# Cross attention with a feature-major product with V, and a head-major forget gate with a running sum

## What is computed

```python
for l in range(DEPTH_2):                                   # 2 layers
    x = x + 0.5 * swiglu(rmsnorm_2(x, g_ffn1[l]), ...)
    h = rmsnorm_2(x, g_mix[l])
    z = h @ w_mix_in[l]                                    # ... and 8 forget columns zf
    log_f = log_sigmoid(zf + b_f[l])
    y_att = forgetting_attention(q, k, v, log_f)           # c = cumsum(log_f) over the tokens
    x = x + y @ w_mix_out[l]
    x = x + memory_cross_attention(rmsnorm_2(x, g_xattn[l]), rmsnorm_2(mem, g_mem[l]), ...)
    x = x + 0.5 * swiglu(rmsnorm_2(x, g_ffn2[l]), ...)

def memory_cross_attention(h, m, w_q, w_kv, w_o):          # 4 heads of 256, 256 memory rows
    s = einsum('bshd,bmhd->bhsm', q, k) * (XHEAD_DIM ** -0.5)
    p = softmax(s, axis=-1)
    o = einsum('bhsm,bmhd->bshd', p, v).reshape(B, S, D_MODEL)
    return o @ w_o
```

## Time and profile before

| | |
|---|---|
| median of 3 runs | 1566.6 us (1564.68 to 1567.84) |
| profiled execution | 1566.79 us, of which the span from first to last instruction is 1564.5 us |
| mean granted TensorE clock | 0.993 of 2.4 GHz |
| PE busy | 1541.5 us (99% of the span) |
| PEld busy | 1349.5 us (86%) |
| DVE busy | 967.6 us (62%) |
| ACT busy | 756.3 us (48%) |
| POOL busy | 50.2 us (3%) |

### The profile page before, as it was taken

The page is one execution under the profiler, slowest core; times in us unless marked ns, Lnnn a source line. Parts: engine busy times, 40 slices in busy tenths (PEclk is TensorE's granted clock), DMA queues, the critical chain, the costliest instruction groups (busy, mean ns, idle before and its releaser), DMA issues.

```text
span 1564.5 us, 22731 instructions
## 1 busy us (share of the span) xinstructions
PE 1541.5 (99%) x8810; PEld 1349.5 (86%) x8810; DVE 967.6 (62%) x992; ACT 756.3 (48%) x839; POOL 50.2 (3%) x76
## 2 busy tenths in 40 slices
PE   9999999999999999999999999999999999999997
PEld 8888888888888899989888887888899989888886
DVE  4556766657665745765666666666664666476665
ACT  5544544446444534544544445444445444364444
POOL 0210000000000000000100000000000000000000
PEclk9999999999999999999999999999999999999999
DMA  9544455455555454343455554555544354255552
GB/s 364 191 153 176 159 190 193 180 188 194 196 181 196 148 213 162 135 162 135 162 188 188 188 188 171 203 179 198 192 168 182 120 177 174 97 183 193 181 194 108
DMA packets 39640, 279.57 MB, mean 179 GB/s; under 512 B 4368, under 2 KB 4624, under 8 KB 6160
## 3 DMA queue, kind: packets, MB, share of 16 engines
q1 hardware_dynamic: 38848, 275.27, 48.4%
q10 hardware_dynamic: 720, 3.29, 0.6%
HBM read 277.49 MB, written 1.05 MB: 178 GB/s over the span
## 4 chain that ended last, share of the span: by engine, by line
PE 97%; DVE 1%; issue 1%; DMA 0%; ACT 0%; POOL 0%; POOLq 0%; ACTq 0%; DVEq 0%
PE ps L338 95%; PE ps L523 2%; PE ps L553 0%; DMA res<-x_in 0%; DVE res L1436 0%; DVE Pb L1416 0%; PE ps L532 0%; DVE PTb L1413 0%; PE ps L513 0%; ACT Pb L1226 0%; DVE qk_tok L1775 0%; POOL stat L1805 0%; DVE Vx L1383 0%; DVE xmax L1757 0%; PE ps L850 0%
## 5 line engine op out<-in xcount | busy, mean ns | idle before, releaser
L1257 DVE TENSOR_TENSOR w_lo<-raw,w_hi 128x2048 fp32r<-128x2048 f32 x252 | 576.4, 2291 | 321.1 <-ACT w_hi L889 320.7
L338 PE MATMUL ps<-xT,w_hi 128*128 128x512 f32 (+1 forms) x2984 | 727.7, 345 | 0.0
L889 ACT ACTIVATE w_hi<-raw 128x2048 fp32r<-128x2048 f32 (+1 forms) x255 | 484.6, 1900 | 361.3 <-PE ps L338 347.7
L338 PEld LDWEIGHTS ps<-xT,w_hi 128*128 128x128 f32 x2984 | 478.9, 191 | 20.8
L338 PE MATMUL ps<-xT,w_lo 128*128 128x256 f32 x2304 | 478.5, 281 | 0.0
L338 PEld LDWEIGHTS ps<-xT,w_lo 128*128 128x128 f32 x2304 | 409.0, 190 | 53.8
L338 PE MATMUL ps<-w_hi,sT_hi 128*128 128x512 f32 x576 | 185.8, 391 | 0.8 <-DVE Vx L1383 0.8
L338 PE MATMUL ps<-w_hi,xT 128*128 128x512 f32 (+2 forms) x640 | 186.3, 385 | 0.0
L338 PE MATMUL ps<-w_lo,sT_hi 128*128 128x512 f32 x576 | 184.9, 390 | 0.0
L338 PE MATMUL ps<-w_hi,sT_lo 128*128 128x512 f32 x576 | 184.8, 390 | 0.0
L338 PEld LDWEIGHTS ps<-w_hi,xT 128*128 128x128 f32 x640 | 118.1, 193 | 24.3 <-issue 1.3
(11 more groups left out here) (165 smaller groups left out, 848.3 us busy)
## 6 DMA issues: line engine op xcount, KB each, us to landing
raw<-stream_in SPq DMA_DIRECT2D x256, 1024.0 KB, 4.8
kTx<-mem_in ACTq DMA_DIRECT2D x2, 1024.0 KB, 6.5
res<-x_in SPq DMA_DIRECT2D x2, 512.0 KB, 5.8
kTx<-mem_in SPq DMA_DIRECT2D x1, 1024.0 KB, 9.3
cu<-gate_bias_in SPq DMA_DIRECT2D x1, 1024.0 KB, 14.5
qk_tok<-post_gain_in ACTq DMA_DIRECT2D x1, 1024.0 KB, 5.0
out<-Vx SPq DMA_DIRECT2D x2, 512.0 KB, 3.1
cst<-consts_in SPq DMA_DIRECT2D x1, 512.0 KB, 7.7
```

The source lines that it names most:

```text
L338: return nc.tensor.matmul(bank_ap, lh, rh, start=start, stop=stop)
L889: nc.scalar.activation(w_hi[:, slot(c), 0:width], raw[:, slot(c), 0:width], copy).then_inc(unit_hi, 1)
L1257: nc.vector.tensor_tensor(w_lo[:, slot(c), :], raw[:, slot(c), :], w_hi[:, slot(c), :].bitcast(F32), sub).then_inc(unit_lo, 1)
```

## The change

In the cross attention the probabilities are divided by their sums before they are transposed (`x_norm` on DVE: one reciprocal of two columns and two in-place multiplications of 128 x 256 a head), the product with V puts out features by tokens straight into the banks 0 to 3 (`x_values`: V stationary, 256 tokens moving, again 16 float32 products), and `turn(xq_tok)`, `xo0`, `xo1` and the tile `xq_tok` are gone. `turn_round` and `turn_rest` read the banks 0 to 3, and the `tall` units and `onto_res` use the banks 4 to 7. The work of the heads is interleaved on PE and DVE. ACT copies the heads 2 and 3 to `PTb`, DVE the heads 0 and 1.

In the forget gate the weights become the stationary operand: ACT writes the 8 rounded columns of each row block at steps of 64 in `w_hi`, DVE the rest 32 columns behind, and 16 products with 256 tokens moving give heads by tokens in bank 4 (rounded weights in partitions 0 to 7, rests in 32 to 39). The bias becomes a column (`bcol`). The elementwise steps run on 8 partitions x 256 tokens, in `PTb`. The sum over the tokens is a `tensor_tensor_scan` on DVE (`cum`), and the two products with `upto` are gone. `cT` is set to zero once at the start.

The name of the change also speaks of a merged gate/up; `merged` stands in the kernel before already, and the diff does not touch it.

PE:

```diff
@@ -678,6 +691,7 @@
+            pe.wait_ge(set_ready, 3)
             with pe.Fori(0, LAYERS) as l:
@@ -737,16 +751,10 @@
                 pe.wait_ge(unit_lo, upto_unit(L3, m0 + 4))
-                fw = w_hi[:, slot(m0 + 4), 0:F_COLS].rearrange("p (k n) -> p k n", k=KT)
                 for k in range(KT):
-                    for t in range(TOK):
-                        def hi_pass(o=ps[:, 4 + t, 0:2 * HEADS], x_=xT_hi[:, k, t * P:(t + 1) * P]):
-                            return mm(o, x_, fw[:, k, :], k == 0, k == KT - 1)
-                        if k < KT - 1:
-                            hi_pass()
-                        last = mm(ps[:, 4 + t, 0:HEADS], xT_lo[:, k, t * P:(t + 1) * P], fw[:, k, 0:HEADS], False, False)
-                        if k == KT - 1:
-                            last = hi_pass()
+                    fw = w_hi[:, slot(m0 + 4), k * F_STEP:k * F_STEP + P]
+                    mm(ps[:, 4, 0:S], fw, xT_hi[:, k, :], k == 0, False)
+                    last = mm(ps[:, 4, 0:S], fw, xT_lo[:, k, :], False, k == KT - 1)
                 last.then_inc(unit_used, 1)
...
                 flipped(L3, m0 + 7, 0, B)
-                wait_dve("logf")
-                mm(ps[:, 6, 0:S], nlf[:, 0, :], upto, True, False)
-                mm(ps[:, 6, P:S], nlf[:, 1, :], upto[:, 0:P], False, True).then_inc(l_pe.sem, l_pe.one("cT"))
                 flipped(L3, m0 + 8, 1, B)
                 wait_dve("cT")
...
+                def x_turn(h):
+
+                    wait_dve(f"xn{h}")
                     for m in range(2):
                         for t in range(TOK):
                             last = nc.tensor.transpose(ps[:, 4 + h, m * S + t * P:m * S + (t + 1) * P],
                                                        Pb[:, h, t * S + m * P:t * S + (m + 1) * P], ident)
                     last.then_inc(l_pe.sem, l_pe.one(f"PX{h}"))
...
-                                last = mm(ps[:, 2 * half + t, e * XDH:(e + 1) * XDH],
-                                          PTb[:, h, m * S + t * P:m * S + (t + 1) * P],
-                                          Vx[:, m, h * XDH:(h + 1) * XDH], m == 0, m == 1)
-                    last.then_inc(l_pe.sem, l_pe.one(f"OX{half}"))
-
-                def o_wait(k):
-                    if k % 4 == 0:
-                        wait_dve(f"xo{k // 4}")
-                turn(xq_tok, N, wait=o_wait)
+
+                def x_values(h):
+
+                    if h < 2:
+                        wait_dve(f"PX{h}")
+                    else:
+                        wait_act(f"PX{h}")
+                    for d in range(2):
+                        for m in range(2):
+                            last = mm(ps[:, h, d * S:(d + 1) * S], Vx[:, m, h * XDH + d * P:h * XDH + (d + 1) * P],
+                                      PTb[:, h, m * S:(m + 1) * S], m == 0, m == 1)
+                    last.then_inc(turn_T, 1)
+
+                x_scores(0)
+                x_scores(1)
+                x_scores(2)
+                x_turn(0)
+                x_scores(3)
+                x_turn(1)
+                x_values(0)
+                x_turn(2)
+                x_values(1)
+                x_turn(3)
+                x_values(2)
+                x_values(3)
                 tl = turns_before(l, 4)
                 for i in range(4):
-                    tall(L3, m0 + 29 + i, 2 * i, 0, i == 0, i == 3, xT_hi, xT_lo, tiles=tl)
+                    tall(L3, m0 + 29 + i, 2 * i, 4, i == 0, i == 3, xT_hi, xT_lo, tiles=tl)
```

ACT:

```diff
-                wait_pe("cT")
-                did(nc.scalar.activation(cT[:], ps[:, 6, 0:S], copy), "cT_hi")
+                wait_dve("cum")
+                did(nc.scalar.activation(cT[0:HEADS, :], f_cum[0:HEADS], copy), "cT_hi")
...
-                for h in (0, 2):
+                for h in (2, 3):
                     wait_pe(f"PX{h}")
                     did(nc.scalar.activation(PTb[:, h, :], ps[:, 4 + h, :], copy), f"PX{h}")
-                turn_round(turns_before(l, 4), N, None)
+                turn_round(turns_before(l, 4), (0, 1, 2, 3), None)
```

DVE:

```diff
+                did(nc.vector.tensor_tensor_reduce(out=bpick[:], in0=ident[:, 0:HEADS], in1=colsL[:, L_BF:L_BF + HEADS],
+                                                   scale=1.0, scalar=0.0, op0=mul, op1=add, accum_out=bcol[:]), "bcol")
                 unit(5)
...
+                did(nc.vector.tensor_tensor(f_lo[hi], ps[lo, 4, 0:S], inv_row[lo, :], mul), "f_lo")
+                did(nc.vector.tensor_tensor(f_hi[hi], ps[hi, 4, 0:S], inv_row[hi, :], mul), "f_hi")
+                wait_own("f_hi")
+                did(stt(out=f_all[hi], in0=f_hi[hi], scalar=bcol[hi], in1=f_lo[hi], op0=add, op1=add), "f")
                 wait_own("f")
-                did(stt(out=lf[:, 1], in0=lf[:, 0], scalar=-1.0, in1=lf[:, 0], op0=mul, op1=mx), "fabs")
+                did(stt(out=f_abs[hi], in0=f_all[hi], scalar=-1.0, in1=f_all[hi], op0=mul, op1=mx), "fabs")
                 unit(7)
 
                 wait_act("fln")
...
+                did(stt(out=f_neg[hi], in0=f_all[hi], scalar=0.0, in1=f_ln[hi], op0=ALU.min, op1=sub, reverse1=True), "logf")
+                wait_own("logf")
+                did(nc.vector.tensor_tensor_scan(f_cum[hi], ones[hi, 0:1].to_broadcast([HEADS, S]), f_neg[hi], 0.0, mul, add),
+                    "cum")
                 unit(8)
                 unit(9)
                 wait_act("cT_hi")
-                did(nc.vector.tensor_tensor(cT[32:64, :], ps[32:64, 6, 0:S], cT[32:64, :].bitcast(F32), sub), "cT")
+                did(nc.vector.tensor_tensor(cT[lo, :], f_cum[hi], cT[hi, :].bitcast(F32), sub), "cT")
...
+                def x_norm(h):
+
+                    wait_act(f"xexp{h}")
+                    did(nc.vector.reciprocal(rinv[:, h:h + 9:8], soft[:, 1, h:h + 9:8]), f"xr{h}")
+                    wait_own(f"xr{h}")
+                    for t in range(TOK):
+                        pr = Pb[:, h, t * S:(t + 1) * S]
+                        last = nc.vector.tensor_scalar(pr, pr, rinv[:, 8 * t + h:8 * t + h + 1], None, mul)
+                    did(last, f"xn{h}")
...
+                x_shift(0)
+                x_shift(1)
+                x_norm(0)
+                x_shift(2)
+                x_norm(1)
+                x_turned(0)
+                x_shift(3)
+                x_norm(2)
+                x_turned(1)
+                x_norm(3)
+                turn_rest(turns_before(l, 4), (0, 1, 2, 3), None)
                 for i in range(31, 34):
                     unit(i)
-                onto_res(3, (L3, m0 + 32), 0, lambda t: 1.0)
+                onto_res(3, (L3, m0 + 32), 4, lambda t: 1.0)
```

More of the change, by code:

```diff
@@ L44 @@
 F_COLS = KT * 2 * HEADS
+F_STEP, F_LOW = 64, 32
 WARM_X, WARM_FIRST, WARM_NORM = 3, 3, 7
@@ L143, in program @@
         rinv = sb("rinv", [P, 16])
-        lf = sb("lf", [P, 5, TOK, HEADS])
+        bcol = sb("bcol", [P, 1])
+        bpick = sb("bpick", [P, HEADS])
         nlf = sb("nlf", [P, TOK, P])
@@ L164, in program @@
         zbT = zb_tok[:, :, :].rearrange("p t n -> p (t n)").rearrange("p (c n) -> p c n", c=4)
-        xq_tok = qk_tok[:, :, :, :].rearrange("p a t n -> p (a t n)").rearrange("p (t n) -> p t n", t=TOK)
         xqT = qkT[:, :, :, :].rearrange("p a k n -> p (a k) n")
         mem_tok = kTx[:, :, :].rearrange("p k n -> p (k n)").rearrange("p (t n) -> p t n", t=TOK)
+        f_lo, f_hi, f_all, f_abs, f_exp, f_ln, f_neg, f_cum = (
+            PTb[:, i // 2, (i % 2) * S:(i % 2) * S + S] for i in range(8))
         o_tok, ysq = q_tok, k_tok.rearrange("p t n -> p (t n)").rearrange("p (c n) -> p c n", c=4)
@@ L289, in upto_unit, with forget_cols, forget_raw @@
             return r3 * RING + c + 1
+        def forget_cols(w, c):
+            return w[:, slot(c), 0:KT * F_STEP].rearrange("p (k n) -> p k n", k=KT)
+        def forget_raw(c):
+            return raw[:, slot(c), 0:F_COLS].rearrange("p (k n) -> p k n", k=KT)[:, :, 0:HEADS]
         @block.sync
@@ L835, in _, with x_scores @@
                 flipped(L3, m0 + 28, 1, B, half_sem=l_pe.sem)
-                for h in range(XH):
+                def x_scores(h):
                     if h == 0:
@@ L1156, in _ @@
                 unit(3)
-                round_unit(L3, m0 + 4, F_COLS)
+                act.wait_ge(unit_landed[slot(m0 + 4)], landed(L3, m0 + 4))
+                used(L3, m0 + 1)
+                nc.scalar.activation(forget_cols(w_hi, m0 + 4)[:, :, 0:HEADS], forget_raw(m0 + 4), copy).then_inc(unit_hi, 1)
                 unit(5)
@@ L1161, in _ @@
                 wait_dve("fabs")
-                did(nc.scalar.activation(lf[:, 2], lf[:, 1], exp, scale=-1.0), "fexp")
+                did(nc.scalar.activation(f_exp[0:HEADS], f_abs[0:HEADS], exp, scale=-1.0), "fexp")
                 act.wait_ge(l_act.sem, l_act.upto("fexp", l))
-                did(nc.scalar.activation(lf[:, 3], lf[:, 2], ACT.Ln, bias=1.0), "fln")
+                did(nc.scalar.activation(f_ln[0:HEADS], f_exp[0:HEADS], ACT.Ln, bias=1.0), "fln")
```

(35 more changed lines are left out.)

37 lines of the change are left out of this document (7 added, 30 removed), and 3 rows, old and new, of the table L_DVE.

## The result

The changed kernel takes 1550.71 us in the median of 4 runs (1547.77 to 1550.93) against 1566.25 us for the kernel before (4 runs, 1564.68 to 1567.84). The ratio is 0.9895, with a 95% interval of 0.9884 to 0.9907. The forecast was 1551.0 us. The profiled execution is the fastest of the four, 1547.77 us with a span of 1546.0 us, 18.5 us shorter than the span before. The other three take 3 us more; their mean granted clocks, 0.995 to 0.997 against 0.996, do not explain it, and none of them was profiled. Experiment 9 ran the same kernel again and took 1548.65 us in the median.

A forecast was written before the change was run, and what follows sets the result against it. PE was taken to bound the kernel, with 97% of the chain that ended last. The terms 6.3 + 3.3 + 4.9 + 1.3 = 15.8 us, off the profiled 1566.8 us, gave 1551.0 us; range 1547.5 to 1556.5.

The forecast's parts named there:

- Cross attention: Stage from first score to first `tall`: 16.01 us instead of 19.16, 3.15 us less a layer, 6.3 us in all.
- upper bound of 3.4 us a layer: Cross-attention stage: the gain without any wait of PE or cost for changing the kind of product, 3.4 us.
- Forget products: Forget block: 16 products in 1.92 us instead of 32 in 3.59; 1.67 us saved a layer, 3.3 in all.
- The clock: Behind the forget block: the fall to 1.2 GHz goes, saving 1.65 us in layer 0 and 3.25 in layer 1, 4.9.
- The sum over tokens: Forget gate: the two products with `upto` go, 0.65 us a layer, 1.3 in all; the scan is costed at nothing.
- 6.6 was counted: Forget gate: about 6.6 us left for DVE's scan after `logf` before PE would feel it.
- the clock falls all the same: Rival, behind the new forget block: the fall in clock and its 4.9 us stay, 1555.9 us; chance 0.12.
- DVE's chain: Rival, cross attention: transposes wait for DVE's divisions, some 1.5 us a layer stay as new waits, 1554.0 us; chance 0.10.
- its rival: Start of layer 1: pause or clock differs, about 1548.0 us if the clock holds, 1554 to 1557 with second pause; chance 0.08.
- The slower rival: Forget gate: the scan is far slower than elementwise, costing beyond 6.6 us; at 17 us the kernel takes 1571.8; chance 0.02.

The follow-up runs named there:

- experiment 9: The changed kernel itself run once more, with no edit, on the same chip as the version with the load moved: 1548.65 us.
- Experiment 1: The kernel before with only the cross-attention part of the change, forget gate as before: 1559.5 us, ratio 0.9958.
- experiment 3: The kernel before with each of the forget block's 32 products streaming 256 columns instead of 16 or 8: 1560.93 us, ratio 0.9967.
- Experiment 2: The kernel before with only the forget-gate part of the change, cross attention as before: 1556.06 us, ratio 0.994.
- experiment 6: The changed kernel with one idle reduction of 9216 elements on DVE ahead of the scan: 1557.97 us, ratio 0.9948.
- experiment 7: The changed kernel with an idle reduction of 384 elements on DVE ahead of each of the four cross-attention divisions: 1554.0 us, one execution.

## Why the prediction was right

The time, 1551.0 against 1550.71 us, is right, and its terms hold up one by one, with one mis-sized. That it is right to 0.3 us is luck: the cross attention gave 0.8 us more than its term, the start of layer 1 moved by 1.65 us without the change, and the same kernel took 1548.65 us in experiment 9.

- **Cross attention, 6.3 us forecast, 7.1 measured.** The turn is gone, and the scores and the products with V together took 13.80 us where 13.90 was read from the earlier trace rows: 7.08 instead of 6.90 and 6.72 instead of 7.00. Mis-sized was the price of what came: four groups of transposes cost 1.80 us instead of 1.96, and PE waited 0.0 instead of 0.15 us for the first division. The prediction had added 0.05 us for each change between kinds of product, which only the first group showed, and something for a wait, which was not there: 15.60 us, not 16.01. Even its upper bound of 3.4 us a layer was passed, by 0.16 us. Experiment 1 confirms the term in the kernel's time.
- **Forget products, 3.3 us.** 16 products to the next unit take 1.92 us, as forecast (12.83 us for the stretch less the 10.88 of 48 wide products is 1.95). That the columns are not what was paid is shown by experiment 3, where 256 columns instead of 16 or 8 cost 0.17 us a layer. The rule of about 25 ns from start to start of small products (the Trainium skill, "TensorE: Matmul & The Clock Gate", "Wait — 56ns, not 53.3ns?"), by which this part would have been a loss, is a floor far below what this trace has: 112 ns a product in a stream in which each loads its own stationary operand.
- **The clock, 4.9 us.** It came off whole, 1.65 and 3.25 us in the profiled execution of before. Experiment 2 shows that the forget part alone does it, experiment 3 that the columns are the cause. What the prediction did not say: the size of the loss in the kernel before varies from run to run, so 4.9 us is what one execution had. Experiment 1's profile has 3.2 us in both layers. Nor is the fall always behind the block, as it says: in layer 1 of before part of the loss lies in the small products themselves, 5.07 us for 33 instead of 3.97.
- **The sum over tokens, 1.3 us.** The two products are gone. The scan's 0.68 us lie in the forecast range of 0.5 to 1 us, and its cover is 7.5 us where 6.6 was counted (experiment 6). The gain of 1.3 us was not run alone, but the traces leave room for just it: in layer 1, from the start of the forget block to the first `tall`, 1347.46 - 1166.82 = 180.64 us before and 1328.81 - 1157.27 = 171.54 after differ by 9.10 us, and 4.90 of the forget stretch and 3.55 of the cross attention leave 0.65.
- **The sum.** Read from the traces the terms are 7.1 + 8.2 (the stretches of the forget block, 3.29 + 4.90) + 1.3 = 16.6 us, and 1.65 us at the start of layer 1 make 18.25 of the 18.5 us between the two spans. The medians differ by 15.5: the profiled execution after was the fastest of four, and the other three took 3 us more, for which no profile shows a cause.

**The rivals.** That the clock falls all the same is out: it stayed at 1.00 in the middle of both layers. DVE's chain did not become the bound, but experiment 7 shows how little was missing; with 0.47 us more a head, 0.97 us a layer would have stayed. The start of layer 1 did differ in the profiled execution, as its rival said it might, by 1.65 us and not the 3 that it put down. The slower rival is priced by experiment 6: a delay behind `logf` begins to cost at 7.5 us, and the scan takes 0.68.

## What to carry to other kernels

Where PE is busy all the time, look at its granted clock in windows of a few microseconds and not at a page's tenths: a short block of products with few columns moving cost 3.6 us at the full clock, and the fall that it caused up to 3.3 us more, in the block and behind it. Make the thin operand the stationary one, or, where that can't be, give the products more columns: experiment 3 gained 5.3 us by adding work. The division that was moved ahead of the transposes stayed hidden only with the heads interleaved, and a load of 1 MB issued just ahead of the loop's jump back cost 3.6 us, so it is worth trying such a load elsewhere.

## What the runs showed of the hardware

256 moving float32 columns in the rounded format cost hardly more than 16 or 8 when each product loads a new 128 x 128 operand: 3.76 us for 32 products against 3.59. A block of 32 products with 16 or 8 columns, with PE never idle, brought the clock from 2.4 to 1.2 GHz in both layers of both profiles that have it; with 256 columns the clock held. A scan of 256 elements on 8 partitions takes 0.68 us, 1.6 times the 0.42 of an elementwise step of that size. And the pause "issue" at the jump back of a loop was 1.7 us in the two profiles without a 1 MB load in the DMA engines and 3.1 to 3.6 us in the nine with it. With the longer pause the clock fell to its low level late in it or right behind it in all but one (experiment 7's, where it fell only later, at 960 us, during another wait), with the shorter one in neither of two.
